# Depthwise convolution: six of eight tiles over four token phases on TensorE, with matrices made by GpSimd a stage earlier

## The reference, cut to what matters

```
for i in range(DEPTH):                                # DEPTH = 2
    h = swiglu(rmsnorm(x, norm_pre[i, 0]), w1, w3, w2)        # ffn0 / ffn2
    x = x + 0.5 * rmsnorm(h, norm_post[i, 0])
    h = rmsnorm(x, norm_pre[i, 1])
    h = s5_mixer(h, ...) if i == 0 else conv_mixer(h, ...)    # s5 / conv
    x = x + rmsnorm(h, norm_post[i, 1])
    h = swiglu(rmsnorm(x, norm_pre[i, 2]), w1, w3, w2)        # ffn1 / ffn3
    x = x + 0.5 * rmsnorm(h, norm_post[i, 2])

def conv_mixer(h, w_in, b_in, dw, dw_b, ln_g, ln_b, w_out, b_out):
    z = h @ w_in + b_in                               # 1024 -> 2048
    a, g = jnp.split(z, 2, axis=-1)
    z = a * jax.nn.sigmoid(g)
    z = causal depthwise convolution of z with dw, 31 taps, + dw_b
    z = jax.nn.silu(layernorm(z, ln_g, ln_b))
    return z @ w_out + b_out
```

## Time and profile before

| | us |
|---|---|
| median of 3 runs (2986.99 to 2992.73) | 2988.04 |
| profiled execution | 2989.68 |
| its span, first to last instruction | 2987.0 |
| PE busy | 2789.5 (93%) |
| DVE / ACT / POOL busy | 1590.9 / 1131.3 / 542.5 |
| rstd of ffn2 / conv / ffn3 (L493) | 1967.05 / 2350.06 / 2618.1 |

### The profile page before, as it was taken

The page is one execution under the profiler, slowest core; times in us unless marked ns, Lnnn a source line. Parts: engine busy times, 40 slices in busy tenths (PEclk is TensorE's granted clock), DMA queues, the critical chain, the costliest instruction groups (busy, mean ns, idle before and its releaser), DMA issues.

```text
span 2987.0 us, 36682 instructions
## 1 busy us (share of the span) xinstructions
PE 2789.5 (93%) x13972; PEld 2302.0 (77%) x13972; DVE 1590.9 (53%) x2286; ACT 1131.3 (38%) x1884; POOL 542.5 (18%) x463
## 2 busy tenths in 40 slices
PE   6998989999999999999689999999999996999998
PEld 5766778767788888888578888888888884888887
DVE  4478655677565432665355443354432897544423
ACT  3347643376443422312343222332222556432222
POOL 1020431112367600134120000110000213200000
PEclk8996999988999999987799999999999997999999
DMA  3320013200143423432222223322223110132232
GB/s 133 99 71 1 15 59 103 80 29 1 36 95 130 132 86 94 136 76 72 79 77 85 92 86 87 101 85 94 88 87 96 57 57 29 57 99 87 87 97 68
DMA packets 292398, 234.79 MB, mean 79 GB/s; under 512 B 43683, under 2 KB 286060, under 8 KB 291756
## 3 DMA queue, kind: packets, MB, share of 16 engines
q1 hardware_dynamic: 289180, 219.49, 24.1%
q10 hardware_dynamic: 2016, 7.46, 0.8%
q0 software_dynamic: 1072, 6.10, 0.5%
HBM read 220.83 MB, written 12.19 MB: 78 GB/s over the span
## 4 chain that ended last, share of the span: by engine, by line
PE 79%; DVE 9%; issue 4%; ACT 4%; POOLq 2%; DVEq 1%; POOL 1%; SPq 0%; DMA 0%; ACTq 0%
PE bank L385 23%; PE bank L383 23%; PE bank L384 22%; DVE WL L369 2%; PE bank L1626 2%; ACT WH L364 1%; PE bank L1604 1%; DVE stats L1984 1%; PE bank L1638 1%; DVE XL L443 1%; PE bank L1132 1%; POOLq L2439 1%; POOLq L2437 1%; PE bank L1134 1%; PE bank L1133 1%
## 5 line engine op out<-in xcount | busy, mean ns | idle before, releaser
L383 PE MATMUL bank<-XH,WH 128*128 128x512 f32 (+1 forms) x2496 | 933.9, 374 | 65.5 <-DVE WL L369 25.5
L385 PE MATMUL bank<-XH,WL 128*128 128x512 f32 (+1 forms) x2496 | 929.2, 372 | 0.0
L384 PE MATMUL bank<-XL,WH 128*128 128x512 f32 (+1 forms) x2496 | 923.0, 370 | 0.0
L369 DVE TENSOR_TENSOR WL<-raw,WH 128x2048 fp32r<-128x2048 f32 (+1 forms) x212 | 447.8, 2112 | 562.6 <-ACT WH L364 562.3
L383 PEld LDWEIGHTS bank<-XH,WH 128*128 128x128 f32 x2496 | 480.0, 192 | 159.1 <-DVE WL L369 36.8
L364 ACT ACTIVATE WH<-raw 128x2048 fp32r<-128x2048 f32 (+1 forms) x212 | 369.9, 1746 | 532.3 <-PE bank L385 532.3
L384 PEld LDWEIGHTS bank<-XL,WH 128*128 128x128 f32 x2496 | 480.4, 192 | 91.7 <-issue 3.3
L385 PEld LDWEIGHTS bank<-XH,WL 128*128 128x128 f32 x2496 | 478.9, 192 | 82.0
L385 PE MATMUL bank<-HH,WL 128*128 128x512 f32 (+1 forms) x792 | 295.3, 373 | 0.0
L384 PE MATMUL bank<-HL,WH 128*128 128x512 f32 (+1 forms) x792 | 292.3, 369 | 0.0
L383 PE MATMUL bank<-HH,WH 128*128 128x512 f32 (+1 forms) x792 | 291.9, 369 | 0.0
(11 more groups left out here) (404 smaller groups left out, 3908.0 us busy)
## 6 DMA issues: line engine op xcount, KB each, us to landing
raw<-in_ffn_w_dram SPq DMA_DIRECT2D x88, 1024.0 KB, 5.3
raw<-in_ffn_w_dram SPq DMA_DIRECT2D x64, 704.0 KB, 4.7
raw<-in_w_in_dram SPq DMA_DIRECT2D x24, 1024.0 KB, 5.2
raw<-in_w_out_dram SPq DMA_DIRECT2D x8, 1024.0 KB, 5.2
raw<-in_cv_w_in_dram SPq DMA_DIRECT2D x8, 1024.0 KB, 5.4
cs_scr<-CSA ACTq DMA_DIRECT2D x8, 520.0 KB, 3.0
raw<-in_w_mem_kv_dram SPq DMA_DIRECT2D x4, 1024.0 KB, 5.2
raw<-in_s_w_in_dram SPq DMA_DIRECT2D x4, 1024.0 KB, 7.9
```

What stands on the lines that cost most here:

```text
L369: dve.tensor_tensor(WL[:, slot, 0:n * P], raw[:, slot, 0:n * P], WH[:, slot, 0:n * P].bitcast(F32), ALU.subtract).then_inc(l_done, 1)
L383: pe.matmul(out, WH[:, slot, c:c + P], h, start=start, stop=False)
L384: pe.matmul(out, WH[:, slot, c:c + P], l, start=False, stop=False)
L385: return pe.matmul(out, WL[:, slot, c:c + P], h, start=False, stop=stop)
```

## The change

The conv stage no longer divides the taps of each tile. Tiles 0 and 1 go to DVE altogether (60 steps, alternating between the two, in pieces between its other work); tiles 2 to 7 go to PE altogether. There the 512 tokens are divided into four phases (token n = 4 i + phase). DVE writes z of such a tile by phases into `ZS`; 16 DMAs on SP's queue move it into `PZ`, whose partitions hold 4 phases x 32 channels, for four groups of channels. A banded matrix then does the taps of several tokens at once: 36 matmuls of 128x128x128 in plain fp32 per tile (L1278). ACT evicts to `PO` (L1317), 16 DMAs on SP bring it back to `CP`, ACT adds the bias and puts the tokens in order into `CV` (L1323).

The matrices (12, two a tile, 128 x 2304, 1.18 MB each) are made in ffn2: ACT makes `WT` and `EYE` in 20 small copies, POOL multiplies them, both broadcast, and stores each matrix to `mm_scr` in DRAM by a DMA of its own queue, which waits for the landing of the one before. ACT waits for all 12 after pair 4 of ffn2, since `HH` from tile 11 on takes their place in SBUF. SP loads them again in the conv stage into four slots `MM`.

The norm subtracts a provisional mean of five tiles (2, 3, 0, 1, 4) as tiles arrive, sums the squares, and the last three centred tiles, on PE, and corrects: variance = mean square minus square of the mean's rest. Sqrt and reciprocal become Ln and Exp; the rest of the mean is taken off by DVE (4 tiles) and POOL (4).

```diff
+        def shifted_act(act, s):
+            taps = dwT[:, :].rearrange("p (t k) -> p k t", k=KD)
+            act.wait_ge(ss(s, "zpad"), 1)
+            for ph in range(PH):
+                rows = slice(ph * PW_, (ph + 1) * PW_)
+                act.activation(EYE[rows, :], ident[rows, rows], ACT.Copy)
+                for g in range(4):
+                    ins = act.activation(WT[rows, :, g, 5 - ph:5 - ph + CONV_W],
+                                         taps[g * PW_:(g + 1) * PW_, TILES_P[0]:, :], ACT.Copy)
+            ins.then_inc(ss(s, "wt"), 1)
...
+            for m in range(NM):
+                n, half = m // 2, m % 2
+                w = WT[:, n, 2 * half:2 * half + 2, :].rearrange("p g q -> p (g q)")
+                pool.tensor_tensor(MB[m % SLOTS_M], w.unsqueeze(2).to_broadcast(shape),
+                                   EYE[:, :].unsqueeze(1).to_broadcast(shape), ALU.mult).then_inc(ss(s, "diag"), 1)
+                pool.wait_ge(ss(s, "diag"), at(s, "diag", m + 1))
+                if m >= 1:
+                    pool.wait_ge(ss(s, "mat_out"), 16 * m)
+                pool.dma_start(mm_scr[m], MB[m % SLOTS_M]).then_inc(ss(s, "mat_out"), 16)
...
+            elif matrix_stage(s):
+                for i in range(1, 5):
+                    pair(i, 16)
+                act.wait_ge(ss(s, "mat_out"), 16 * NM)
...
+            def to_phases(k):
+                n = k - TILES_P[0]
+                sp.wait_ge(ss(s, "z"), at(s, "z", k + 1))
+                if n >= 1:
+                    sp.wait_ge(ss(s, "u_in"), at(s, "u_in", 16 * PH * 4 * n))
+                for g in range(4):
+                    for ph in range(PH):
+                        sp.dma_start(PZ[ph * PW_:(ph + 1) * PW_, n, g, LEAD:], ZS[g * PW_:(g + 1) * PW_, k % 2, ph, :])\
+                          .then_inc(ss(s, "u_in"), 16)
...
+            def from_phases(k):
+                n = k - TILES_P[0]
+                sp.wait_ge(ss(s, "po"), at(s, "po", n + 1))
...
+                for g in range(4):
+                    for ph in range(PH):
+                        q = PH - 1 - ph
+                        sp.dma_start(CP[g * PW_:(g + 1) * PW_, n % 3, ph, :], PO[q * PW_:(q + 1) * PW_, n % 2, g, :])\
+                          .then_inc(ss(s, "y_out"), 16)
...
+            def matrices(m):
+                if m >= SLOTS_M:
+                    sp.wait_ge(ss(s, "ptap"), at(s, "ptap", m - SLOTS_M + 1))
+                if m >= 2:
+                    sp.wait_ge(ss(s, f"scr_in{m % 2}"), SCR_IN + 16 * (m // 2))
+                sp.dma_start(MM[:, m % SLOTS_M], mm_scr[m]).then_inc(ss(s, f"scr_in{m % 2}"), 16)
...
+            matrices(9)
+            from_phases(4)
+            to_phases(6)
+            to_phases(7)
+            matrices(10)
+            matrices(11)
+            from_phases(5)
+            out_block(2)
+            from_phases(6)
+            out_block(3)
+            from_phases(7)
...
+            n = k - TILES_P[0]
...
+            pe.wait_ge(ss(s, "u_in"), at(s, "u_in", 16 * PH * 4 * (n + 1)))
+            if n >= 3:
+                pe.wait_ge(ss(s, "po"), at(s, "po", n - 2))
+            for half in range(2):
+                m = 2 * n + half
+                pe.wait_ge(ss(s, f"scr_in{m % 2}"), SCR_IN + 16 * (m // 2 + 1))
+                for g in (2 * half, 2 * half + 1):
+                    for j in range(9):
+                        c = (g % 2) * NQ + j * PH
+                        mm = pe.matmul(acc[:, g * NS:(g + 1) * NS],
+                                       MM[:, m % SLOTS_M, c:c + PH, :].rearrange("p q c -> p (q c)"),
+                                       PZ[:, n, g, j:j + NS], start=(j == 0), stop=(j == 8))
+                mm.then_inc(ss(s, "ptap"), 1)
...
-                    in_pair(pe, s, b0, j0)
-                    continue
-                pe_block256(pe, b0 + 2 * i, 0, j0 + 4 * i, XH, XL)
-                pe_block256(pe, b0 + 2 * i + 1, 1, j0 + 4 * i + 2, XH, XL)
-                if i >= 1:
-                    taps_pe(pe, s, 2 * i - 2)
-                    taps_pe(pe, s, 2 * i - 1)
-            taps_pe(pe, s, KD - 2)
-            taps_pe(pe, s, KD - 1)
-            pe.wait_ge(ss(s, "cvsum"), at(s, "cvsum", KD))
+            in_pair(pe, s, b0, j0)
...
+            act.activation(rcol[:, 0, 0:1], eps_c[:, 0:1], ACT.Ln)
+            evict(5)
             act.wait_ge(ss(s, "cvstat"), at(s, "cvstat", 1))
...
+            act.activation(rms[:, :], stat[:, :], ACT.Copy, scale=1.0 / (P * len(FIRST))).then_inc(ss(s, "mu"), 1)
+            back(5)
+            for n in range(len(FIRST)):
+                square_c(n)
+            evict(6)
+            square_c(5)
+            back(6)
+            square_c(6)
+            evict(7)
+            back(7)
+            square_c(7)
+            act.wait_ge(ss(s, "censum"), at(s, "censum", 1))
+            act.activation(work1[:, 0, :], bank[6][:, :], ACT.Copy, scale=1.0 / D)
+            act.activation(work1[:, 1, :], bank[6][:, :], ACT.Square, scale=1.0 / D).then_inc(ss(s, "mu"), 1)
...
             dve.wait_ge(ss(s, "mu"), at(s, "mu", 1))
-            for k in range(KD):
-                dve.tensor_tensor(CV[:, k, :], CV[:, k, :], rms[:, :], ALU.subtract).then_inc(ss(s, "cen"), 1)
-            dve.wait_ge(ss(s, "sigma"), at(s, "sigma", 1))
-            dve.reciprocal(rstd[:, :], rms[:, :])
+            for n in range(KD):
+                centre(n)
+            dve.wait_ge(ss(s, "mu"), at(s, "mu", 2))
+            dve.wait_ge(ss(s, "censtat"), at(s, "censtat", KD))
+            dve.scalar_tensor_tensor(work2[:, 0, :], stat[:, :], 1.0 / D, work1[:, 1, :], ALU.mult, ALU.subtract)\
+               .then_inc(ss(s, "var"), 1)
+            for k in range(4):
+                dve.tensor_tensor(CV[:, k, :], CV[:, k, :], work1[:, 0, :], ALU.subtract)
...
+            for k in range(KD):
+                if k >= 4:
+                    dve.wait_ge(ss(s, "csub"), at(s, "csub", k - 3))
+                dve.tensor_tensor(CV[:, k, :], CV[:, k, :], rms[:, :], ALU.mult).then_inc(ss(s, "nrm"), 1)
+                if k >= 2:
+                    low(k - 2)
+            low(KD - 2)
+            low(KD - 1)
```

More of the change, by code:

```diff
@@ L187, in program @@
         rb.close()
+        rb = ExitStack()
+        sb("mh_low", [P, F0, T], F32, rb)
+        MBA = sb("MBA", [P, 2, 72, 32], F32, rb)
+        WT = sb("WT", [P, 6, 4, 36], F32, rb)
+        EYE = sb("EYE", [P, 32], F32, rb)
+        sb("mh_top", [P, (KF - F0) * T - 2 * 72 * 32 - 6 * 4 * 36 - 32], F32, rb)
+        sb("ml_low", [P, F0, T], F32, rb)
+        MBB = sb("MBB", [P, 2, 72, 32], F32, rb)
+        rb.close()
+        MB = [x[:, i] for x in (MBA, MBB) for i in range(2)]
         def tables(x):
@@ new lines, in matrices @@
+            def matrices(m):
[4 more added lines that the diff above has]
+                sp.dma_start(MM[:, m % SLOTS_M], mm_scr[m]).then_inc(ss(s, f"scr_in{m % 2}"), 16)
+            for n in range(4):
+                in_block(n)
+            sp.wait_ge(mm_done, first_step[s])
+            for m in range(3):
+                matrices(m)
@@ new lines, in conv_sp @@
+            in_block(4)
+            in_block(5)
+            matrices(3)
+            in_block(6)
+            to_phases(2)
+            to_phases(3)
+            in_block(7)
+            out_block(0)
+            matrices(4)
+            matrices(5)
+            from_phases(2)
+            to_phases(4)
+            to_phases(5)
+            out_block(1)
+            matrices(6)
+            matrices(7)
+            from_phases(3)
+            matrices(8)
+            matrices(9)
+            from_phases(4)
@@ L1155, in conv_pe @@
-            taps_pe(pe, s, KD - 1)
-            pe.wait_ge(ss(s, "cvsum"), at(s, "cvsum", KD))
-            pe.matmul(stat[:, :], ones[:, :], ssq[:, :], start=True, stop=True).then_inc(ss(s, "cvstat"), 1)
-            pe.wait_ge(ss(s, "censum"), at(s, "censum", KD))
-            pe.matmul(stat[:, :], ones[:, :], ssq[:, :], start=True, stop=True).then_inc(ss(s, "censtat"), 1)
+            in_pair(pe, s, b0, j0)
+            for n in range(2, 8):
+                pe_block256(pe, b0 + n, n % 2, j0 + 2 * n, XH, XL)
+                if n >= 4:
+                    taps_pe(pe, s, n - 2)
@@ L1180, in conv_act @@
                        .then_inc(ss(s, "sig"), 1)
[L1181 to L1185, removed]
-                    act.activation(CV[:, k, :], ZP[:, k, last:last + T], ACT.Identity, bias=col("cv_dw_b_2", k),
-                                   scale=dwT[:, last * KD + k:last * KD + k + 1]).then_inc(ss(s, "cva"), 1)
@@ L1205, in conv_act, with ahead @@
-            act.activation(rms[:, :], stat[:, :], ACT.Sqrt, bias=eps_c[:, 0:1], scale=1.0 / D)\
-               .then_inc(ss(s, "sigma"), 1)
+            def ahead(n):
+                split_h(act, b0 + n, n % 2, 16, s0 + 2 * n - 2)
+            sigmoids(0)
+            ahead(3)
+            for k in TILES_D:
+                act.wait_ge(ss(s, "z"), at(s, "z", k + 1))
```

(22 more changed lines are left out.)

239 lines of the change are left out of this document (144 added, 95 removed).

## The result

The kernel with the change takes 3031.8 us (3030.3 to 3035.2, four runs), beside 2989.4 for the kernel before: the ratio is 1.014, interval 1.0128 to 1.0153. The forecast ratio was 0.997, and the forecast range ended at 2999. Both stages that the change touches came out worse than the sum had them. The profiled execution has a span of 3028.7, 41.7 more than before.

| stage | before | with the change | forecast |
|---|---|---|---|
| start of ffn2 | 1967.05 | 1965.37 | |
| ffn2, to the rstd of conv | 383.0 | 416.2 (+33.2) | +15 |
| conv, to the rstd of ffn3 | 268.0 | 278.0 (+9.9) | -22.5 |

What follows compares the result with a forecast made beforehand. PE, busy 93% of the span, was taken to bound the kernel, with a chain of short steps ending the conv stage. Conv -22.5 us plus ffn2 +15 us gave -7.5, so 2980 us against 2988.0, range 2963 to 2999.

Steps and rivals of the forecast that it cites:

- the sum: Whole kernel: conv stage -22.5 us and ffn2 +15 us, together -7.5 us; chance 0.42.
- Rival C: ffn2: POOL's tensor_tensor takes 5.9 to 6.9 us each, net +8.5 to +18.5 us, 2996.5 to 3006.5; chance 0.15.
- The path of the prediction: Conv stage: from the first matmul, PE blocks, SP's queue and the norm's end in series, 158.3 us to the first product.
- block 7 done: Conv stage, PE: 6 blocks (67.1 us) and the taps of tiles 2, 3 and 4 (24.3) end at 91.4 us.
- z of 6 and 7, SP ready for them: Conv stage, behind block 7: z of tiles 6 and 7 takes 2 us before SP moves them to phases.
- 32 issues and a landing: Conv stage: SP moves tiles 6 and 7 to phases, 32 issues at 0.38 us and 1.9 us to land.
- matrices 10, 11 and the way back of 5: Conv stage: loading 2.36 MB at 5.4 us a MB takes 12.7 us and hides the 16 issues for tile 5.
- back 5, squares: Conv stage: tile 5 back, its centring and five squares, later ones each waiting for a sum on PE: 6.5 us.
- end of the norm: Conv stage: last stat matmul to first product, 11.9 us now, less 3.35 for the reciprocal, plus 3.9: 12.4 us.
- the prediction's own signs of being wrong: ffn2 as long as before, issues costing 0.5 us, or PE's waits for the phases beginning already at tiles 2 to 5.
- Rival B: Conv stage: SP's queue is slower, 0.45 us per issue and late landings; -12 + 15 = +3 us, 2991; chance 0.20.
- Rival D: Conv stage: plain fp32 tap matmuls cost 0.47 us each, as at half clock; 53 us more on PE, around 3010; chance 0.06.

Runs made afterwards that it cites:

- e2: The changed kernel with each POOL multiplication of 2304 elements in ffn2 issued as eight of 288, same work: 3025.0 us.
- e5: Against e2: POOL waits for each of the eight pieces to complete before it issues the next; 3011.9 us.
- e8: The changed kernel with copies on POOL, matrices started at chosen places, phases by way of DRAM with 5 DMAs a turn, tile 6 evicted earlier: 2952.8 us.
- e1: The changed kernel with POOL multiplying only 9 of 72 columns of each matrix, after a memset of its four buffers; stores and copies stay: 3004.1 us.

## Why the prediction was wrong, point by point

**The matrices, ffn2: +33.2 in place of +15.** The mechanism was right, from the earlier trace rows: a two-input operation of DVE waits for POOL's. So was the price of a matrix, 4.08 to 5.19 us for the 4.3 from the earlier trace rows. Rival C, slower by a dearer tensor_tensor, thus had the direction right by luck: its cause is absent. Three steps failed.
1. The count. The step went "the second L943 for the second, the second HH is done, split_h ends, and split_l meets the third matrix". Between them DVE's queue holds two more two-input operations, HL of both tiles, one matrix each: 10.07 us. They stood in the list of the stage's operations, and I left them out of the chain. The matrices that the two HL met put the start of split_l at 1995.5, not 1989.4, though its input WH was ready at 1988.1. Split_l ended 36.8 us behind the rstd, forecast 24.6; 4.1 of the 12.2 are the next item, some 8 this one.
2. The copies: 0.57 us for each of WT, not 0.29. The nearest row was a 128x128 activation with a pace of 0.3; a WT copy has 186 elements on 32 partitions and stands 0.57 from the next. The 20 gave 9.9 us, not 5.8. (The rest of the 33.2: 3.9 us in the second pair for the 2 of the sum, and by difference some 5 in place of 1.5 for the clock, which is 0.50 in the 10 us ahead of 1995 and again from 2030.1 to 2034.)
3. "DVE waits for the one of POOL that is running." It can be held past that one, until a gap in POOL's queue (e2, e5). With whole matrices the two are alike, since the store makes a gap behind each. That ffn0 told so little may come from the same: POOL's many operations there often wait for their own results, and most are 1 to 2 us long. No run tests that.

**conv: +9.9 in place of -22.5.** The path of the prediction, with what each step took; the stretch from the first matmul (2383.06) to the first product (2575.50) was 192.4 us, forecast 158.3:

| step | forecast | measured |
|---|---|---|
| block 7 done | 91.4 | 93.7 |
| z of 6 and 7, SP ready for them | 2 | 16.5 |
| 32 issues and a landing | 14.1 | 22.1 |
| matrices 10, 11 and the way back of 5 | 12.7 | 12.4 |
| back 5, squares | 6.5 | 6.3 |
| evict 6 | 1.3 | 0.6 |
| 16 issues, landing | 8.0 | 11.2 |
| back 6, square, evict 7 | 2.0 | 3.1 |
| 16 issues, landing | 8.0 | 11.3 |
| end of the norm | 12.4 | 15.3 |

The issue price (0.63 for 0.38), with the landings, is 14.5 of the 34 us; an issue at 0.5 was one of the prediction's own signs of being wrong. The earlier trace rows had given 0.38 from the first loads and a median of 0.43 for y_scr; but 0.43 is how long such an issue lasts, and in the same trace its starts mostly lie 0.47 apart. None of those was a DMA within SBUF, and the range didn't allow for that. As much, 14.5, is a step that was missing altogether: at the end of block 7 the queue still had the ways back of tiles 3 and 4 ahead of it (10.76 and 10.24 us in the rows above; at 0.38 an issue they too would have been shorter, so the two causes are not quite apart). Until tile 3's had landed, ACT stood in `back` and gave no sigmoid for tiles 6 and 7:

```profile
2481.25 1.22 ACT L1323 ACTIVATE CV<-CP,vecT 128x512 f32<-128x512 f32 x1 [21.59 <-DMA CP<-PO]
2482.27 0.63 ACT L1317 ACTIVATE PO<-bank 128x512 f32<-128x512 f32 x1
2482.80 1.31 ACT L1337 ACTIVATE SG<-work,vecT 128x512 f32<-128x512 f32 x2
```

I had counted the queue from block 7 on as if it were empty. The fourth row of the table is right by luck: matrix 10 had landed by 2520.87, when the taps of tile 7 began, and the 12.4 us are the two issues, the 16 issues of the way back, hidden in the forecast, and their landing. PE was late by its own path as well: its taps of tile 7 ended at 2530.70, and the third square waited for it:

```profile
2531.66 0.63 ACT L1330 ACTIVATE sq<-CV 128x512 f32<-128x512 f32 x1 [1.68 <-PE bank L1301]
```

The whole queue, 192 issues of 0.63 = 121 us in a stretch of 150, would have shown it, and at 0.38 it would have been 73. Rival B had the mechanism of the price and too low a price; it had neither ffn2 nor the missing step. (The range is said to end at the start of C, at 2999, where C's own sum starts at 2996.5; nothing hangs on it.)

**The end of the norm** took 2.9 more than forecast. There the same thing as in ffn2 happens: DVE's and POOL's halves of the correction run against each other, four DVE subtractions in 6.03 us in place of 2.8. POOL's four are issued without a wait between them, and DVE gets in behind each, as in the first pair of e2:

```profile
2566.32 6.03 DVE L1463 TENSOR_TENSOR CV<-CV,work 128x512 f32<-128x512 f32 x4
```

**What held.** The tap matmuls of tiles 2 to 5 take 8.2 to 8.3 us a tile (8.1); the first output tile comes 10.5 us behind the first product (10.6); the last matrix was issued for storing at 2040.40, ahead of ACT's wait. Rival D had almost no part in it: only the taps of tiles 6 and 7 ran at a low clock, 4.6 us more for the two. In e8 the conv stage, with its taps on PE over phases and its new norm, is 34 us shorter than before: the change had that gain and paid it away.

The Trainium skill (SBUF — State Buffer, section "SBUF: two separate sides") says of the port pair that the loser is held for the whole instruction, and, for a DVE operation with two SBUF inputs, only beside a GpSimd operation that reads SBUF. The 4.32 us beside a matrix and the 0.69 beside the memset of e1 agree. Two things differ, and there the measurement decides: in e2 DVE was held for eight operations in a row, and the part of the rule that the prediction quotes, that whoever starts first has the ports, doesn't come out of the recorded starts. This split_l starts 0.43 us ahead of a matrix and ends 2.2 us behind it (DVE, then POOL); whether a recorded start is the moment at which the ports are taken no run shows:

```profile
2023.39 6.68 DVE L382 TENSOR_TENSOR WL<-raw,WH 128x2048 fp32r<-128x2048 f32 x1
```
```profile
2023.82 4.09 POOL L737 TENSOR_TENSOR MBA<-WT,EYE 128x2304 f32<-128x2304 f32 x1
```

## What to carry to other kernels

Count the instructions of a queue over the whole stretch, not along one path: a queue of 192 small DMAs is an engine with 121 us of work, and a hop by DRAM with 5 DMAs beat 16 without it. Take the price of an issue from the distance between two starts, not from the duration of one. Before giving idle GpSimd a long operation, list every VectorE operation with two SBUF inputs up to the next thing that TensorE waits for, and let GpSimd wait for a place behind them; cutting it in pieces gained nothing sure here until it waited between the pieces. And two small costs on two engines can do more than add up: the copies with an eighth of the matrices' work cost 9.7 us, the matrices without copies on ACT 9.7, both 33.2.

## What the runs showed of the hardware that was not expected

- Pieces of a POOL operation issued back to back can hold DVE as one: two HL 12.06 us (e2), 2.77 with a wait between the pieces (e5). They don't always: in the first pair of e2 DVE got in behind one piece (0.99 us).
- A POOL memset doesn't hold DVE: 0.69 us beside 3.5 us of it (e1).
- Small DMAs on SP's queue start 0.63 us apart within SBUF (16 KB each), 0.46 from SBUF to DRAM (16 KB), 0.47 to 0.50 for 64 KB of it; those within SBUF start 0.49 apart on POOL's queue. What makes the first loads of the program cheaper (0.38) stays open.
- A copy of 32x186 on ACT stands 0.57 us from the next, no less than on POOL (2.3 us for four on either); one of 32x32 takes 0.21 to 0.23 on ACT.
